# Experts ranked on the chip by token count; the three with the fewest get 64 slots instead of 96

## The reference

```python
logits = (h @ moe_router[i]).astype(jnp.float32)
top_val, top_idx = lax.top_k(logits, TOP_K)          # TOP_K = 2, N_EXPERTS = 8
gate = jax.nn.softmax(top_val, axis=-1)
weight = jnp.einsum('...k,...ke->...e', gate, one_hot(top_idx, N_EXPERTS))
for e in range(N_EXPERTS):
    out = out + weight[..., e:e + 1] * swiglu(h, moe_w1[i, e], moe_w3[i, e], moe_w2[i, e])
# swiglu(h, w1, w3, w2) = (silu(h @ w1) * (h @ w3)) @ w2, 1024 -> 2816 -> 1024
```

## Time and profile before

| what | value |
|---|---|
| median of three runs | 1839.01 us |
| the profiled execution | span 1839.6 us, 41949 instructions |
| TensorE matmuls | busy 1771.7 us, 96% of the span |
| line 2100, up matmuls of the experts | 9216 records, 467.9 us |
| line 2121, down matmuls of the experts | 4080 records, 229.1 us |
| loads of expert weights | 280, of which 216 of 1 MB and 64 of 0.75 MB |
| HBM read | 433.81 MB |

### The profile page before, as it was taken

The page is one execution under the profiler, slowest core; times in us unless marked ns, Lnnn a source line. Parts: engine busy times, 40 slices in busy tenths (PEclk is TensorE's granted clock), DMA queues, the critical chain, the costliest instruction groups (busy, mean ns, idle before and its releaser), DMA issues.

```text
span 1839.6 us, 41949 instructions
## 1 busy us (share of the span) xinstructions
PE 1771.7 (96%) x19374; PEld 1367.6 (74%) x19374; DVE 696.1 (38%) x950; ACT 423.5 (23%) x582; POOL 52.8 (3%) x61
## 2 busy tenths in 40 slices
PE   7999999998999999998998999999999999999997
PEld 3777676786788888876887886677666897665786
DVE  5457656444433336978655652010100010101013
ACT  4233344333322222215425441000000000000001
POOL 0000000002000001210000010000000000000000
PEclk9999999999999999999999998999999999999998
DMA  9721211235122225772332488999999999999992
GB/s 377 301 101 46 107 58 47 69 126 211 69 91 91 97 94 214 254 277 105 134 108 69 140 354 353 376 418 401 388 386 413 409 405 392 376 407 403 415 404 86
DMA packets 66414, 440.26 MB, mean 239 GB/s; under 512 B 7537, under 2 KB 7793, under 8 KB 22850
## 3 DMA queue, kind: packets, MB, share of 16 engines
q1 hardware_dynamic: 60482, 404.19, 56.2%
q0 software_dynamic: 4976, 30.70, 4.5%
q10 hardware_dynamic: 784, 2.75, 0.4%
HBM read 433.81 MB, written 3.80 MB: 238 GB/s over the span
## 4 chain that ended last, share of the span: by engine, by line
PE 88%; DVE 7%; issue 3%; ACT 2%; DMA 0%; DVEq 0%; ACTq 0%; SPq 0%
PE psum L2100 25%; PE psum L1613 14%; PE psum L1615 13%; PE psum L1614 13%; PE psum L2121 12%; PE psum L1660 1%; PE psum L2076 1%; ACT units_hi L644 1%; PE psum L1854 1%; PE psum L1876 1%; DVE units_lo L1017 1%; PE psum L1643 1%; DVE squares L1100 1%; PE psum L1864 1%; PE psum L1834 1%
## 5 line engine op out<-in xcount | busy, mean ns | idle before, releaser
L2100 PE MATMUL psum<-expert_units,gathered 128*32 128x256 f32 (+1 forms) x9216 | 467.9, 361 | 4.6 <-issue 4.3
L2100 PEld LDWEIGHTS psum<-expert_units,gathered 128*32 128x32 f32 x9216 | 345.3, 110 | 121.7 <-issue 8.2
L1613 PE MATMUL psum<-h_hi,units_hi 128*128 128x512 f32 (+1 forms) x928 | 344.5, 371 | 13.1 <-DVE h_lo L1088 6.2
L1615 PE MATMUL psum<-h_hi,units_lo 128*128 128x512 f32 (+1 forms) x928 | 336.0, 362 | 0.0
L1614 PE MATMUL psum<-h_lo,units_hi 128*128 128x512 f32 (+1 forms) x928 | 335.9, 362 | 0.0
L1017 DVE TENSOR_TENSOR units_lo<-raw_units,units_hi 128x2048 fp32r<-128x2048 f32 (+2 forms) x88 | 175.1, 1990 | 269.0 <-ACT units_hi L644 269.0
L644 ACT ACTIVATE units_hi<-raw_units 128x2048 fp32r<-128x2048 f32 (+2 forms) x88 | 147.2, 1673 | 405.8 <-PE psum L1615 350.9
L2121 PE MATMUL psum<-expert_units,expert_midT 128*32 128x256 f32 x4080 | 229.1, 379 | 0.1
L1613 PEld LDWEIGHTS psum<-h_hi,units_hi 128*128 128x128 f32 x928 | 176.4, 190 | 54.8 <-issue 22.9
L2121 PEld LDWEIGHTS psum<-expert_units,expert_midT 128*32 128x32 f32 x4080 | 159.1, 110 | 62.9 <-issue 1.4
L1615 PEld LDWEIGHTS psum<-h_hi,units_lo 128*128 128x128 f32 x928 | 176.4, 190 | 27.1
(11 more groups left out here) (307 smaller groups left out, 1697.6 us busy)
## 6 DMA issues: line engine op xcount, KB each, us to landing
expert_units<-in_moe_up SPq DMA_DIRECT2D x128, 1024.0 KB, 9.8
expert_units<-in_moe_w SPq DMA_DIRECT2D x88, 1024.0 KB, 9.8
expert_units<-in_moe_up_rest SPq DMA_DIRECT2D x64, 768.0 KB, 7.9
raw_units<-in_w_in SPq DMA_DIRECT2D x40, 1024.0 KB, 4.8
raw_units<-in_ffn_w SPq DMA_DIRECT2D x22, 1024.0 KB, 4.8
mod_units<-in_w_mod_rows POOLq DMA_DIRECT2D x20, 1024.0 KB, 7.8
raw_units<-in_ffn_w SPq DMA_DIRECT2D x16, 704.0 KB, 5.3
raw_units<-in_w_pab SPq DMA_DIRECT2D x16, 512.0 KB, 3.3
```

The source lines that it names most:

```text
L1613: MM(o, wh, xh, start=first, stop=False)
L1615: return MM(o, wl, xh, start=False, stop=last)
L2100: ins = MM(o[GRP * q:GRP * (q + 1), :], G[:, k, at, GRP * rr:GRP * (rr + 1)], W[:, kk, q, :], start=k == 0 and rr % 2 == 0, stop=k == DK - ...
```

## The change

The experts are now worked through in eight places. Place 0 is always expert 0, since its weights are loaded before the counts are known. The other seven are ranked by their count on the chip: the three with the fewest tokens go to places 1, 4 and 7 (`SHORT`), the other four to places 2, 3, 5 and 6. A short place has 64 slots, so two groups of 32: `rounds(g, e)` gives 2 there and 3 elsewhere, in the first pass only. The weights are the same 35 units per place; from place 1 on, SyncE reads the number of the expert from SBUF and addresses the units by it. A short place's down projection lays the four quarters out otherwise (`down_part`): two groups of slots times two blocks of 256 output columns at a time, so that two sweeps cover 1024 columns. The flag for passes 2 and 3 is now set if a count exceeds 96, or if a short place's count exceeds 64. With the counts above the short places hold 49, 55 and 62 tokens, and the largest of the others is 82.

```diff
+SHORT = (1, 4, 7)
+LONG_FROM = len(SHORT)
...
+        def rounds(g, e):
+
+            return 2 if g == 0 and e in SHORT else ROUNDS
+
+        def slots(g, e):
+
+            return GRP * rounds(g, e)
...
+        def down_part(g, e, rr, q):
+
+            rows = slice(GRP * q, GRP * (q + 1))
+            if rounds(g, e) == 2:
+                return PS[rows, 4 + rr, 0:BLK], q % 2, 2 * rr + q // 2, True
+            s, c = (q, rr) if q < 3 else (rr, 3)
+            return part_out(4, rr, BLK)[rows, :], s, c, rr % 2 == 0
...
+            def expert_unit(w, e, u):
+
+                return w[bass.ds(e, 1), u].rearrange("o p c -> (o p) c") if e is not None else w[0, u]
+
             def experts(g):
+                at_place_of = {0: None}
                 for e, kind, r in SEQ:
+                    if e not in at_place_of:
+                        if e == 1 and g == 0:
+                            sp.wait_ge(order_ready, 1)
+                        at_place_of[e] = sp.value_load(order_i[0:1, e:e + 1], min_val=0, max_val=NE - 1)
+                    who = at_place_of[e]
...
-                            into, src = ering[n % RING][:], t["moe_w2"][e, 4 * r + u]
+                            into, src = ering[n % RING][:], expert_unit(t["moe_w2"], who, 4 * r + u)
...
             tokens_lo(0)
+            dve.wait_ge(r_cnt, 1)
+            link(STT(key[:], PS[:, 4, 0:NE], float(NE), place_key, ALU.mult, ALU.add))
+            link(TT(below[:], key[:].unsqueeze(1).to_broadcast(square), key[:].unsqueeze(2).to_broadcast(square), ALU.is_lt))
+            link(V_.tensor_reduce(place_of[:], below[:], AX, ALU.add))
+            link(TT(at_place[:], place_of[:].unsqueeze(1).to_broadcast(square), place_at.unsqueeze(2).to_broadcast(square), ALU.is_equal))
             mod_out(1, MTRIPS - 1)
...
+            by_place(rank_at[:], rank[:])
+            link(TT(late[:], rank_at[:], short_from.unsqueeze(1).to_broadcast([P, 2, NE]), ALU.is_ge))
+            link(STT(rank_at[:], late[:], float(GRP), rank_at[:], ALU.mult, ALU.add))
...
+                link(TS(over[:], place_of[:], LONG_FROM - 0.5, float(GRP), ALU.is_lt, ALU.mult))
+                link(TT(over[:], over[:], PS[:, 4, 0:NE], ALU.add))
+                link(V_.tensor_reduce(over[:, 0:1], over[:], AX, ALU.max))
...
+                def short_half(rr, c):
+
+                    a, rows = (2 * rr + c) * BLK, slice(2 * GRP * c, 2 * GRP * (c + 1))
+                    return TT(YO[0:2 * GRP, a:a + BLK], PS[rows, 4 + rr, 0:BLK], gate_rows[rows, a:a + BLK], ALU.mult)
...
-                            for rr in range(ROUNDS):
+                            for rr in range(rounds(g, e)):
                                 o = part_out(bank, rr, w)
```

More of the change, by code:

```diff
@@ L87, in units_of, with rows_before @@
     return 3 if kind == "down" and r == 2 else 4
+def rows_before(e):
+    return sum(CAP - GRP * (p in SHORT) for p in range(e))
 FIRST = {s_: sum(units_of(*q_[1:]) for q_ in SEQ[:i_]) for i_, s_ in enumerate(SEQ)}
@@ L285, in build @@
         row_root = at("row_roots", 161.9375, [P, 2])
+        key = at("place_keys", 162.0, [P, NE])
+        place_of = at("places", 162.03125, [P, NE])
+        order_f = at("expert_order_f", 162.0625, [P, NE])
+        order_i = at("expert_order", 162.09375, [P, NE], mybir.dt.int32)
+        rank_at = at("rank_by_place", 162.125, [P, 2, NE])
+        late = at("rank_is_late", 162.1875, [P, 2, NE])
+        below = at("keys_below", 127.5, [P, NE, NE])
+        at_place = at("expert_at_place", 127.75, [P, NE, NE])
+        spread = at("by_place", 128.0, [P, 2, NE, NE])
         sil = at("expert_silu", 149.5, [P, ROUNDS, BLK])
@@ L1414, in _, with by_place, expert_order @@
             link(TT(rank[:], rank[:], PS[:, 5, 0:2 * NE].rearrange("p (c e) -> p c e", c=2), ALU.add))
+            def by_place(dst, src):
+                link(TT(spread[:], src.unsqueeze(2).to_broadcast(twice), at_place[:].unsqueeze(1).to_broadcast(twice), ALU.mult))
+                link(V_.tensor_reduce(dst, spread[:], AX, ALU.add))
+            by_place(rank_at[:], rank[:])
+            link(TT(late[:], rank_at[:], short_from.unsqueeze(1).to_broadcast([P, 2, NE]), ALU.is_ge))
+            link(STT(rank_at[:], late[:], float(GRP), rank_at[:], ALU.mult, ALU.add))
+            def expert_order():
+                link(TT(below[:], at_place[:], iot[:, 0:NE].unsqueeze(1).to_broadcast(square), ALU.mult))
+                link(V_.tensor_reduce(order_f[:], below[:], AX, ALU.add))
+                V_.tensor_copy(order_i[:], order_f[:]).then_inc(order_ready, 1)
             def gate_weights():
+                for c in range(2):
+                    by_place(oh[:, c, 0:2, :], oh[:, c, 0:2, :])
                 dve.wait_ge(r_ev, 1)
@@ L1490, in gated @@
                         dve.wait_ge(rows_sent, 16 * e)
+                    if rounds(g, e) == 2:
+                        for rr in range(2):
+                            for c in range(2):
+                                last = short_half(rr, c)
+                        last.then_inc(e_y, 1)
+                        return
                     TT(YO[0:CAP, 0:3 * BLK].rearrange("p (r f) -> p r f", r=3), up_out(4, BLK)[0:CAP],
@@ L1497, in parted @@
                 def parted(e):
-                    s = scatters_before(g, e)
+                    s, rows, short = scatters_before(g, e), slots(g, e), rounds(g, e) == 2
                     def low(i):
@@ L2116, in down @@
                             k = 2 * u + kk
-                            for rr in range(ROUNDS):
-                                o = part_out(4, rr, BLK)
+                            for rr in range(rounds(g, e)):
                                 for q in range(4):
-                                    s, c = (q, rr) if q < 3 else (rr, 3)
-                                    ins = MM(o[GRP * q:GRP * (q + 1), :], midT[:, k, GRP * s:GRP * (s + 1)], W[:, kk, c, :],
-                                             start=r + k == 0 and rr % 2 == 0, stop=r == 2 and k == 5, skip_group_check=True)
+                                    o, s, c, first = down_part(g, e, rr, q)
+                                    ins = MM(o, midT[:, k, GRP * s:GRP * (s + 1)], W[:, kk, c, :],
+                                             start=r + k == 0 and first, stop=r == 2 and k == 5, skip_group_check=True)
                         ins.then_inc(e_use, 1)
@@ L2250, in link, with place_order @@
         self.eng.wait_ge(self.sem, self.n if self.i is None else self.n + self.per * self.i)
+def place_order():
+    rising = iter(range(LONG_FROM, NE - 1))
+    short = iter(range(LONG_FROM))
+    return [NE - 1] + [next(short) if e in SHORT else next(rising) for e in range(1, NE)]
 def tables():
@@ L2344 @@
             features_first(a["norm2_g"], 1), features_first(a["hy_conv_w"], 2),
-            features_first(a["hy_conv_b"], 1), tab["lone"], np.tile(np.concatenate([CAP * np.arange(NE), np.where(np.arange(NE) < NE - 1, CAP, 0)]), (P, 1)),
+            features_first(a["hy_conv_b"], 1), tab["lone"], np.tile(np.concatenate([[rows_before(e) for e in range(NE)], np.where(np.arange(NE) < NE - 1, CAP, 0), np.r_[10000, np.arange(1, NE)],
+                                    place_order(), np.where(np.isin(np.arange(NE), SHORT), 2 * GRP, 1e6)]), (P, 1)),
             np.moveaxis(a["moe_router"][0].reshape(DK, P, NE), 1, 0))], axis=1).astype(np.float32),
```

75 lines of the change are left out of this document (44 added, 31 removed).

## The result

| | median us | runs | against before |
|---|---|---|---|
| before, on the same chip | 1839.08 | 4 | |
| changed kernel | 1794.22 (1791.20 to 1796.03) | 4 | ratio 0.9759, 95% interval 0.9745 to 0.9773 |
| forecast | 1794, range 1787 to 1822 | | 45 us faster |

The change gained 44.9 us, 2.4%. The profiled execution of the changed kernel has a span of 1789.3 us and took 1791.20 us, the shortest of the four.

A forecast was written before the change was run, and what follows sets the result against it. TensorE bounds the expert stage, transfers close behind; after the change DMA bytes set its end. 1186 us, 2.0 ranking, 587.8 for 246.6 MB, 0.9 and 16.9 of tail sum to 1793.6, forecast 1794 us, range 1787 to 1822.

The forecast's parts named there:

- The lead of the ring: Expert loads: 9 to 10 of 14 slots are a lead; place 1 uses about all, TensorE waits from place 4 on.
- The sum: Whole timeline: 1186 + 2.0 + 587.8 gives last landing 1775.8 us; plus 0.9 and 16.9 gives 1793.6 us.
- eight instructions before the first gather: Ranking on VectorE before the first selection: eight small instructions at 0.25 us, all on the path, 2.0 us.
- the 86.4 us: TensorE in the three short places: a third of the matmuls of three experts removed, about half of it gained.
- my sign of 35 to 50 us: Places 4 to 7: TensorE's waits released by expert loads should sum to 35 to 50 us.
- Costs at nothing: SyncE's register addressing and expert-number reads: hidden by issued units in flight; without that cover 5 us.
- the three order instructions: VectorE behind the selection: hidden in front of a copy before which VectorE sat idle 2.80 us.
- (a): Rival, loads: transfers do not reach 420 GB/s throughout; at 400 the time is 1822 us; chance 13%.
- (b): Rival, TensorE: the whole 86.4 us come off, 1755 us, needing 449 GB/s; chance 2%.
- (c): Rival, loads: they become the bound and run worse; register-addressed loads at 385 GB/s give 1846 us; chance 5%.
- (d): Rival, TensorE's clock: places 4 and 7 at 1.2 GHz throughout give 1859 us; chance 5%.
- (e): Rival, flag: it is set and passes 2 and 3 run, 16 more places, about 3100 us; chance 1%.

The follow-up runs named there:

- after_cut: Changed kernel, but from the 15th unit on a 1 MB unit loads only 1536 of its 2048 columns, all matmuls kept: 1750.12 us.
- all_short: Changed kernel with all eight places at 64 slots and the flag looking at 96 only: 1778.90 us.
- fixed_order: Changed kernel with the experts' numbers as constants, so no number is read and no load is addressed by register: 1793.76 us.
- no_short: Changed kernel with no short place, all eight at 96 slots, ranking and register-addressed loads kept: 1839.56 us.
- depth3: Changed kernel with at most 3 loads in flight from the 15th unit on: 1826.67 us.
- short_1_7: Changed kernel with only places 1 and 7 at 64 slots, place 4 at 96 again: 1796.48 us.
- run 16: Not a follow-up run: a verb and a count in (e), where passes 2 and 3 would work through 16 more places; no measured time.
- four_short: Changed kernel with place 0 at 64 slots too, so places 0, 1, 4 and 7 are short: 1781.96 us.

## Why the prediction was right

**The bound moves to the loads.** This is shown by after_cut (44 us come back when the loads shrink), by the 31.8 us of waits for landings, and by all_short.

**The lead of the ring.** I said that place 1 uses up the lead and TensorE waits from place 4 on. The waits for landings sum to 0.2 us up to 1285 us and 0.5 up to 1365, and there is none up to 1429 us, where the up matmuls of place 4 start; 11.4 us follow up to 1660 us, and 20.0 behind it. The steps of 29.0, 14.1 and 2.3 us say the same without a trace.

**The sum.** Its terms against the changed trace:

| term | predicted | measured |
|---|---|---|
| eight instructions before the first gather | 2.0 us | 2.0 us (the gather's wait from 0.61 to 2.63 us) |
| bytes behind the point where the loads bound | 246.6 MB behind 1188 us | 246.7 MB behind 1180 us |
| their time | 587.8 us at 419.5 GB/s | 591 us, 417 GB/s in the mean |
| last unit to the scaling | 0.9 us | 1.1 us |
| scaling to the end | 16.9 us | 17.2 us |

The third row hides two errors. With eleven loads in flight the rate is 424 and not 419.5 GB/s, which is 6 us less than I counted; the half-empty 16 us at the end take that back and 3 us more. I had taken the DMA engines for one server, and the sixteen steps of a load come at unequal pace. That the mean rate came out near 419.5 is luck: I had read it in stretches with four to five loads in flight.

The agreement to a fraction of a microsecond is luck too. The profiled execution of before reached the router's choice at 1104.2 us and that of the changed kernel at 1096.6, in a part of the program that is the same in both; the eleven other kernels of this study lie between 1098.3 and 1103.3. From that point to the end the two take 735.4 and 692.7 us, 42.8 us less, where my sum gives 46.0. I also took it that nothing lies around the span, since 1839.6 us lies among the measured times. In every run whose span is on record 1.7 to 2.1 us do, in those of before as well, so the profiled execution of before must have taken some 1841.4 us, more than any of the four measured. The errors are 3.2 us too much gain, 7.5 us of an earlier start and 1.9 us around the span: 1793.6 + 3.2 - 7.5 + 1.9 = 1791.2, the shortest run, and the median is 3 us above it. The last landing, 1775.8 us in my sum, was at 1770.9 us, mostly by that earlier start. All are within the range but not within the precision of the number. The lower end of my own range was added up wrongly too: 1793.6 - 0.7 - 2 is 1791, not 1788.

**Where the other half of the 86.4 us is.** From the first up matmul to the end of the last down projection, before took 710.8 us (shown above) and the changed kernel 665.8:

```profile
1108.80:1774.60 665.80, 629.02 (x11847) 452.00 (x11847) 72.05 (x120) 23.99 (x39) 4.38 (x5) 1.00 0.98 407
```

That is 45.0 us less. TensorE's idle time rose from 6.6 to 36.8 us, by 30.2; the 31.8 us of waits for landings are all of it. Its busy time fell by only 75.2 us instead of 86.4; 11.2 us of what waiting costs are booked as busy. Most of that is in the bursts: 32 records between two waits take 1.93 us; in the long stream of the earlier trace rows a record takes 20.90 / 384 = 54.4 ns and 32 take 1.74 us. The difference is 0.19 us, and 50 x 0.19 = 9.5 us, an estimate. So the waits alone missed my sign of 35 to 50 us; with the time booked as busy they are 41 to 43.

**Costs at nothing.** Reading the number took 0.26 to 0.47 us, the address instruction 0.04, and fixed_order and no_short find nothing. The copy behind the three order instructions still waited 2.19 us for TensorE.

**The rivals.** (a) needed 400 GB/s; from 1180 us on none of the windows above is under 421 up to the last 16 us. Its mechanism is real, though: depth3 is it, with 401 GB/s and 1827 us beside the 1822 worked out. What kept it away is that a drained ring leaves eleven loads out. (b) needed 449 GB/s, and no slice of the page shows more than 425 in the stage. Of the two ceilings of the Trainium skill ("DMA: Bandwidth & Descriptors", Specifications) beside it, the lower is contradicted here: the rate held for 575 us, 423 GB/s, is above the 358 and under the 435. (c) register-addressed loads are as fast as others. (d) in the changed kernel the clock stayed at 1.00 through all short places: waits of up to 1.8 us between bursts of 1.5 to 1.9 us did not lower it, and in all_short such bursts, with waits of up to 2.2 us, ran for 575 us at 1.00. A single fall near the end, the +3 us of my range, did not come in the changed kernel, but it came in others: in all_short at 1755.3 us, in the second of two bursts of 16 records with waits of 0.9 and 1.0 us before them, in depth3 from 1783.2 us after a wait of 2.3 us, and in short_1_7 from 1778.4 us. The changed kernel had the same two short bursts and no fall, so what decides is not shown. In the case of the Trainium skill that I cited ("TensorE: Matmul & The Clock Gate", HAM oscillation) the clock falls in each wait; its waits take several microseconds, and the changed kernel had none above 1.8 us before its last landing. (e) would have run 16 more places and taken about 3100 us, which did not come.

## What to carry to other kernels

Before taking work off the engine that bounds a stage, price the next bound in its own unit, here bytes over the best sustained rate, and see how far a buffer can carry the difference; beyond that the saving is void, and the first of three equal cuts gave 29 us, the last 2. Once transfers bound, look for stretches in which they idle behind a full buffer, and put the cut there: the short place 0 gave 12 us for nothing else. The busy share of TensorE hardly moved (96 to 95%) while its bound changed; the rate row and the waits for landings did.

## What the runs showed of the hardware that I had not expected

- Loads of 1 MB from one queue, rows of 8 KB: 401 GB/s with three in flight, 420 with five, 423 to 425 with about eleven. Up to five, an issue takes 0.33 us; at eleven it takes 2 us at the median and up to 7.4, so SyncE itself is held in the issue.
- The sixteen steps of a load's semaphore do not come at one pace. Eight run ahead of the other eight: after 575 us without a pause the last load's steps stood in two groups around 1756 and 1770 us, and half of the DMA engines' time was empty for the last 16 us (share 0.49). In four_short the groups of the last load are around 1746 and 1759 us, in all_short around 1744 and 1756. Which engines lag, and why, stays open.
- Smaller loads made the matmul-bound kernel 6.5 us faster (interval 4.2 to 9.6 us). In the profiles TensorE idles 3.5 us less and is busy 1.8 us less; the cause was not found.
- TensorE kept its clock at 1.00 for 560 us while it was busy 78% of the time, with waits of up to 2.2 us; in the last down projection of the same kernel (all_short) the clock fell to 0.50 for 6.8 us.
